# Opening of a two-layer decoder step: prompt rows loaded in four transfers, parameters on two queues and turned second, first block interleaved with the turning

## What is computed

```python
def _rms(x, g):
    y = x * lax.rsqrt(jnp.mean(x * x, axis=-1, keepdims=True) + EPS)
    return y * g
...
h = _rms(x, norm_mix[0])
a, g, mq = jnp.split(h @ w_in_a[0], [C_A, 2 * C_A], axis=-1)
c, st = _causal_dwconv(a * jax.nn.sigmoid(g), ...)      # 31 taps
...
```

## Time and profile before

| what | value |
|---|---|
| median of 3 runs | 1501.5 us (1499.77 to 1501.58) |
| time of the profiled execution | 1501.87 us |
| its span in the trace | 1500.2 us |
| instructions | 28216 |
| PE busy | 1401.7 us (93%) |
| DVE busy | 947.8 us (63%) |
| ACT busy | 584.2 us (39%) |
| POOL busy | 154.8 us (10%) |
| mean granted clock of PE | 0.974 |

### The profile page before, as it was taken

The page is one execution under the profiler, slowest core; times in us unless marked ns, Lnnn a source line. Parts: engine busy times, 40 slices in busy tenths (PEclk is TensorE's granted clock), DMA queues, the critical chain, the costliest instruction groups (busy, mean ns, idle before and its releaser), DMA issues.

```text
span 1500.2 us, 28216 instructions
## 1 busy us (share of the span) xinstructions
PE 1401.7 (93%) x11004; PEld 1332.0 (89%) x11004; DVE 947.8 (63%) x1812; ACT 584.2 (39%) x991; POOL 154.8 (10%) x202
## 2 busy tenths in 40 slices
PE   5899877799999999999999988898999999999997
PEld 5799765599999999999987877777999999999997
DVE  5689987666663565366776657666666536653662
ACT  4644534534431232123556454554443313221332
POOL 2000203222000000000300332220200000000001
PEclk9899987899999999999999999999999999999999
DMA  8112323124222322232322443332332332223222
GB/s 234 43 57 57 104 80 89 30 85 140 85 84 86 97 85 85 85 95 67 111 61 81 129 115 110 85 93 83 101 97 84 86 95 87 84 85 95 86 69 71
DMA packets 223216, 134.89 MB, mean 90 GB/s; under 512 B 7739, under 2 KB 216336, under 8 KB 223063
## 3 DMA queue, kind: packets, MB, share of 16 engines
q1 hardware_dynamic: 214687, 111.32, 26.0%
q0 software_dynamic: 7840, 21.89, 4.9%
q10 hardware_dynamic: 584, 0.23, 0.1%
HBM read 126.19 MB, written 7.85 MB: 89 GB/s over the span
## 4 chain that ended last, share of the span: by engine, by line
PE 75%; DVE 14%; ACT 6%; issue 3%; ACTq 1%; DMA 0%; POOL 0%; DVEq 0%; POOLq 0%
PE acc L532 61%; PE acc L709 3%; DVE conv_out L1727 2%; PE psT L666 2%; DVE softmax_stats L2102 1%; PE psX L666 1%; DVE w_lo L1629 1%; ACT w_hi L1156 1%; PE psX L544 1%; ACT exps L1491 1%; PE acc L544 1%; DVE xa_lo L1664 1%; DVE root_row L1652 1%; DVE psX L2100 1%; DVE turned L1640 1%
## 5 line engine op out<-in xcount | busy, mean ns | idle before, releaser
L532 PE MATMUL acc<-xa_hi,w_hi 128*128 128x272 f32 x1760 | 370.7, 292 | 5.4 <-DVE w_lo L1629 5.4
L532 PE MATMUL acc<-xa_hi,w_lo 128*128 128x272 f32 x1760 | 365.4, 289 | 0.0
L532 PE MATMUL acc<-xa_lo,w_hi 128*128 128x272 f32 x1760 | 364.5, 289 | 0.0
L1156 ACT ACTIVATE w_hi<-w_raw 128x1024 fp32r<-128x1024 f32 (+1 forms) x202 | 206.8, 1024 | 341.6 <-PE acc L532 312.2
L1629 DVE TENSOR_TENSOR w_lo<-w_raw,w_hi 128x1024 fp32r<-128x1024 f32 (+1 forms) x202 | 239.9, 1188 | 80.2 <-ACT w_hi L1156 78.2
L532 PEld LDWEIGHTS acc<-xa_hi,w_hi 128*128 128x128 f32 x1760 | 278.1, 189 | 11.5 <-DVE w_lo L1629 5.9
L532 PEld LDWEIGHTS acc<-xa_lo,w_hi 128*128 128x128 f32 x1760 | 278.2, 190 | 0.0
L532 PEld LDWEIGHTS acc<-xa_hi,w_lo 128*128 128x128 f32 x1760 | 276.3, 190 | 0.0
L532 PE MATMUL acc<-xb_hi,w_hi 128*128 128x272 f32 x896 | 194.3, 298 | 2.0 <-DVE xb_lo L2048 2.0
L532 PE MATMUL acc<-xb_hi,w_lo 128*128 128x272 f32 x896 | 185.8, 289 | 0.0
L532 PE MATMUL acc<-xb_lo,w_hi 128*128 128x272 f32 x896 | 185.3, 288 | 0.0
(11 more groups left out here) (337 smaller groups left out, 1879.9 us busy)
## 6 DMA issues: line engine op xcount, KB each, us to landing
w_raw<-in_w_up SPq DMA_DIRECT2D x88, 512.0 KB, 3.8
w_raw<-in_w_down SPq DMA_DIRECT2D x32, 512.0 KB, 3.9
w_raw<-in_w_in_a SPq DMA_DIRECT2D x14, 512.0 KB, 4.2
w_raw<-in_w_down SPq DMA_DIRECT2D x16, 384.0 KB, 3.4
w_raw<-in_w_kv SPq DMA_DIRECT2D x12, 512.0 KB, 4.0
k_pages<-in_cache_k POOLq DMA_DIRECT2D x96, 64.0 KB, 2.3
v_pages<-in_cache_v SPq DMA_DIRECT2D x96, 64.0 KB, 2.1
w_raw<-in_w_mem_kv SPq DMA_DIRECT2D x8, 512.0 KB, 3.8
```

Source lines behind the costliest of these rows:

```text
L532: last = nc.tensor.matmul(acc[slot][:, c, 0:n], w, x[:, k, c * n:(c + 1) * n], start=(k == 0 and q == 0), stop=(k == kb - 1 and q == 2))
L1156: nc.scalar.activation(whi[:, slot % 2, 0:n], wraw[:, slot, 0:n], ACT.Copy).then_inc(w_hi_ready, 1)
```

## The change

The prompt rows are loaded in four transfers of 256 columns instead of two of 512, each with a semaphore of its own, and the sample rows have one too. Every second of the 16 transfers of `put` is issued by POOL instead of ACT. PE turns the parameters after chunk 0 instead of after chunk 3, and turns chunks 4 to 7 inside step 0: chunk k + 4 before the products of chunk k. DVE alternates copies and low parts. ACT makes all high parts before any square, and its squares 0 to 7 follow w_hi(1).

```diff
@@ SP
-            sp.dma_start(xnat[0:NSA, QB, :], a["x_sample"]...).then_inc(ld_x[0], 16)
-            sp.dma_start(xnat[:, 0:QB, 0:512], x_rows[:, :, 0:512]).then_inc(ld_x[0], 16)
-            sp.dma_start(xnat[:, 0:QB, 512:D], x_rows[:, :, 512:D]).then_inc(ld_x[1], 16)
+            sp.dma_start(xnat[0:NSA, QB, :], a["x_sample"]...).then_inc(ld_xs, 16)
+            for i in range(4):
+                sp.dma_start(xnat[:, 0:QB, i * 256:(i + 1) * 256], x_rows[:, :, i * 256:(i + 1) * 256]).then_inc(ld_x[i], 16)
@@ PE
+            def turn_rows(c):
+
+                if c == 1:
+                    pe.wait_ge(ld_rows, 16 * (sum(1 for x in put[0::2] if x[2] is not None) + 4))
+                    pe.wait_ge(ld_rows2, 16 * sum(1 for x in put[1::2] if x[2] is not None))
+                    b = setup_bank(2)
+                    for i in range(4):
+                        n = min(P, NROW - i * P)
+                        last = nc.tensor.transpose(b[:, i * P:i * P + n], rows[0:n, i, :], ident[0:n, 0:n])
+                    last.then_inc(setup_filled, 1)
+                pe.wait_ge(ld_x[c // 2], 16)
+                b = setup_bank(1 + c + (c >= 1))
                 for i in range(QB):
                     last = nc.tensor.transpose(b[:, i * P:(i + 1) * P], xnat[:, i, c * P:(c + 1) * P], ident)
                 last.then_inc(setup_filled, 1)
...
+            for c in range(AHEAD):
+                turn_rows(c)
+
+            def first_ready(k):
+                if k + AHEAD < KD:
+                    turn_rows(k + AHEAD)
+                xa_ready(0)(k)
+
+            mm_step(0, 0, xa_hi, xa_lo, ready=first_ready)
             model_square_sum("n0")
@@ ACT
-            for r, k, src, done in put:
+            for r, k, src, done in put[0::2]:
...
-            for c in range(PARAMS_AT):
-                act.wait_ge(setup_drained, c + 2)
-                square(xT[:, c, :])
-            act.wait_ge(setup_drained, PARAMS_AT + 2)
+            act.wait_ge(setup_drained, 3)
             for c in range(KD):
-                if c == PARAMS_AT:
+                if c == 2:
                     split_hi(0)
-                if c >= PARAMS_AT:
+                if c >= 1:
                     act.wait_ge(setup_drained, c + 3)
                 scaled_hi(xa_hi, c, xT[:, c, :], pcol("norm_mix", c), xg_hi)
-            for c in range(PARAMS_AT, KD):
-                if c == PARAMS_AT + 2:
-                    split_hi(1)
+            split_hi(1)
+            for c in range(KD):
                 square(xT[:, c, :])
@@ DVE
+            row_copy(0)
+            dve.wait_ge(setup_filled, 3)
+            nc.vector.tensor_copy(pT[:, 0:NROW], psT[:, 0, 0:NROW]).then_inc(setup_drained, 1)
+            row_copy(1)
+            for c in range(2, KD):
+                if c == AHEAD:
+                    split_lo(0)
+                first_low(c - 2)
+                row_copy(c)
+            first_low(KD - 2)
+            first_low(KD - 1)
             split_lo(1)
@@ POOL
+            for r, k, src, done in put[1::2]:
+                if src is not None:
+                    pool.dma_start(rows[r % P:r % P + k, r // P, :], src[done:done + k, :]).then_inc(ld_rows2, 16)
```

More of the change, by code:

```diff
@@ L230, in build @@
         ld_const, ld_rows, ld_state, ld_mem = (sem(n) for n in ("ld_const", "ld_rows", "ld_state", "ld_mem"))
-        ld_x = [sem(f"ld_x{i}") for i in range(2)]
+        ld_xs, ld_rows2 = sem("ld_x_sample"), sem("ld_rows_pool")
+        ld_x = [sem(f"ld_x{i}") for i in range(4)]
         w_loaded = [sem(f"w_loaded{i}") for i in range(4)]
@@ L318, in build @@
         RT = dict(n0=0, mem=1, ln=2, n1=3, n2=4, n3=5)
-        PARAMS_AT = KD // 2
+        AHEAD = 4
         tiles = {}
@@ L425, in _ @@
             x_rows = a["x_prompt"].rearrange("o (i p) n -> (o p) i n", p=P)
-            sp.dma_start(xnat[0:NSA, QB, :], a["x_sample"].rearrange("b t n -> (b t) n")).then_inc(ld_x[0], 16)
-            sp.dma_start(xnat[:, 0:QB, 0:512], x_rows[:, :, 0:512]).then_inc(ld_x[0], 16)
-            sp.dma_start(xnat[:, 0:QB, 512:D], x_rows[:, :, 512:D]).then_inc(ld_x[1], 16)
+            sp.dma_start(xnat[0:NSA, QB, :], a["x_sample"].rearrange("b t n -> (b t) n")).then_inc(ld_xs, 16)
+            for i in range(4):
+                sp.dma_start(xnat[:, 0:QB, i * 256:(i + 1) * 256], x_rows[:, :, i * 256:(i + 1) * 256]).then_inc(ld_x[i], 16)
             def load(s, src, kb=KD):
@@ L580, in setup_bank @@
                 return psT[:, q % 2, :]
-            pe.wait_ge(ld_x[0], 32)
+            pe.wait_ge(ld_xs, 16)
             b = setup_bank(0)
@@ L587, in _, with xa_ready @@
             last.then_inc(setup_filled, 1)
-            for c in range(KD):
-                if c == PARAMS_AT:
-                    pe.wait_ge(ld_rows, 16 * (sum(1 for x in put if x[2] is not None) + 4))
-                    b = setup_bank(1 + c)
+            def xa_ready(n):
+                return lambda k: pe.wait_ge(xg_lo, 8 * n + k + 1)
+            def turn_rows(c):
[3 more added lines that the diff above has]
+                    b = setup_bank(2)
                     for i in range(4):
@@ L595, in _ @@
                     last.then_inc(setup_filled, 1)
-                    pe.wait_ge(ld_x[1], 16)
-                b = setup_bank(1 + c + (c >= PARAMS_AT))
+                pe.wait_ge(ld_x[c // 2], 16)
+                b = setup_bank(1 + c + (c >= 1))
                 for i in range(QB):
@@ L600, in _ @@
                 last.then_inc(setup_filled, 1)
-            def xa_ready(n):
-                return lambda k: pe.wait_ge(xg_lo, 8 * n + k + 1)
-            mm_step(0, 0, xa_hi, xa_lo, ready=xa_ready(0))
+            for c in range(AHEAD):
[5 more added lines that the diff above has]
+            mm_step(0, 0, xa_hi, xa_lo, ready=first_ready)
             model_square_sum("n0")
@@ L1670, in _, with row_copy, first_low @@
                                   ).then_inc(setup_drained, 1)
[L1671 to L1675, removed]
+            def row_copy(c):
+                i = 1 + c + (c >= 1)
                 dve.wait_ge(setup_filled, i + 1)
                 nc.vector.tensor_copy(xT[:, c, 0:NPR], psT[:, i % 2, :]).then_inc(setup_drained, 1)
-            dve.wait_ge(setup_drained, KD + 2)
-            for c in range(KD):
-                if c == PARAMS_AT:
+            def first_low(c):
+                if c == 0:
+                    dve.wait_ge(setup_drained, 3)
+                else:
+                    dve.wait_ge(setup_drained, c + 3)
+                scaled_lo(xa_lo, xa_hi, c, xT[:, c, :], pcol("norm_mix", c), xg_hi, xg_lo, c + 1)
+            row_copy(0)
[4 more added lines that the diff above has]
+                if c == AHEAD:
                     split_lo(0)
-                scaled_lo(xa_lo, xa_hi, c, xT[:, c, :], pcol("norm_mix", c), xg_hi, xg_lo, c + 1)
+                first_low(c - 2)
+                row_copy(c)
+            first_low(KD - 2)
+            first_low(KD - 1)
             split_lo(1)
```

## The result

The changed kernel takes 1510.66 us (median of 4 runs, 1509.47 to 1511.11) against 1500.63 for the kernel before (1499.61 to 1501.58). The ratio is 1.0066, with a 95% interval of 1.0048 to 1.0083: slower by 10.0 us. The profiled execution has a span of 1509.1 us against 1500.2, 8.9 more; its time, 1511.11 against 1501.87, is 9.2 more, so 0.3 us of it lies outside the span.

A forecast was written before the change was run, and what follows sets the result against it. Opening bound by parameter landing, then ACT and DVE, afterwards PE (93% busy). Sum 7.1 us later plus 2.1 for the low clock gives 9.2 on 1501.5: 1510.7 us, range 1505.5 to 1514.5.

The forecast's parts named there:

- The parameters' moment P: When PE's wait for the last parameter transfers ends: 15.23 before, taken as 13, the middle of 10.6 and 15.2.
- the rival with P counting as 10.6: Parameters land soon after issue, at 9.4 to 10.6; step 0's weights then decide; 6.8 us slower, 1508.3; chance 0.2.
- no gain (15.2): Rival: parameters land no earlier than before because queued data decides; 11.4 us slower, 1512.9; chance 0.15.
- its 6.05: Time in us from ACT's issue of the last parameter transfer to its landing in the kernel before.
- From P to the first square: Opening on PE, DVE and ACT, through the high parts until w_hi(1) ends and squares can start: P + 16.05 us.
- The squares' chain: Eight squares on ACT and POOL's additions behind w_hi(1), ahead of PE's sum: 10.65 us.
- The start of the sum: PE's sum over `square_total` between steps 0 and 1 starts at P + 26.7, 39.7 against 32.59: 7.1 us later.
- The sum at the low clock: PE's clock falls while idle, so the sum runs slower (1.9) and step 1 starts slower (0.2): 2.1 us.
- the 0.2 for step 1: Cost in us of step 1's start on PE until the clock is back, 4.2 us after work was taken up.
- What follows is moved as a whole: The stretch from 40.3 to 60 and all after it shift with the sum; nothing there takes the delay up.
- The rival of a better clock behind step 1: Not slower: clock at 1.00 in the stretch 40.3 to 60 shortens it by at most 5.1 us; chance 0.03.
- The price of moved work beside other work: POOL additions cost 1.32 to 1.41 us beside idle or copying DVE, 1.81 beside low parts; allowance -0.5 to +2.4 over six.

The follow-up runs named there:

- Experiment 1: Changed kernel with its squares spread over ACT's idle time in the opening instead of all behind w_hi(1); 1502.13 us, ratio 1.0008 to the kernel before.
- experiment 6: Changed kernel with POOL's second to sixth addition of the first norm cut from 544 to 8 columns; 1504.44 us, ratio 1.0030 to the kernel before.
- experiment 7: Changed kernel with 68 turnings of the identity on PE between step 0 and the sum; 1509.27 us, ratio 1.0058 to the kernel before.
- experiment 2: Kernel before with squares 0 to 7 all behind w_hi(1), nothing else changed; 1507.09 us, ratio 1.0043 to the kernel before.
- experiment 3: Changed kernel with PE's sum of squares behind step 1 instead of ahead of it; 1510.33 us, ratio 1.0064 to the kernel before.
- experiment 8: Changed kernel without late squares: parameters turned behind chunk 3, squares 0 to 3 before high parts, all chunks turned before step 0, DVE reordered; 1495.82 us, ratio 0.9965.
- experiment 5: Changed kernel with all eight chunks turned on PE before step 0, DVE and ACT unchanged; 1508.12 us, ratio 1.0055 to the kernel before.

## Why the prediction was right

The predicted 1510.7 us met 1510.66. The mechanism was right; that the number fits so closely is luck. The kernel before took 1500.63 in this comparison and not the 1501.5 that the prediction stood on, so the difference is 10.0 us (7.2 to 12.5 by the interval) against 9.2 predicted, and terms of the sum offset each other. In the profiled executions it is 6.0 for the later sum, 2.9 behind it and 0.3 outside the span. By its own steps:

- *The parameters' moment P.* Taken as 13, it was 12.83, and 12.2 to 13.1 in the seven experiments that have the change's loads and show PE waiting for them. No row gave it: it was the middle between two bounds, so the fit is luck. The last transfer on ACT was issued within 5.48 + 0.70 and took over 6.6 us to land, so neither early landing (the rival with P counting as 10.6) nor no gain (15.2) came true. Counted as the prediction counts its 6.05 (which is 6.1: 15.23 less 9.1), it took 7.0. The Trainium skill, page "DMA: Bandwidth & Descriptors", section on queues, rings and completion order, says that a DMA engine takes the queues that have work in turn, a packet at a time. The conclusion drawn from it, that P would follow the issue and count as 10.6, isn't borne out by this trace (12.83); what held the transfer no run shows.
- *From P to the first square.* Taken as 16.05 us, it was 15.0 (12.83 to 27.85), which put the sum 1 us too late. The turnings inside step 0 were priced too high: 0.85 each by the earlier trace rows, where four chunks took 3.40, but 0.42, 0.71, 0.71 and 0.36 from one row's start to the next in the changed kernel (19.56, 20.93, 23.15 and 24.78). The products between them took longer than assumed, 3.4 us for three chunks, where the prediction's times leave 2.9. w_lo(0) was done 0.3 us earlier after P than assumed.
- *The squares' chain.* Taken as 10.65 us, it was 10.72 (27.85 to 38.57). Experiment 1, which moves the chain, takes the wait out, and experiment 6, which shortens it, halves it. That the wait is at this chain's end is shown. One remark on it was wrong: not four squares and three additions ran before P in the kernel before, but two squares and one addition. Squares 2 and 3 start at 15.11 and the next two additions at 15.85, so a part of the cover was the turning and copying behind P.
- *The start of the sum.* 39.7 predicted, 38.57 measured: 6.0 us later than before, not 7.1.
- *The sum at the low clock.* This term was mis-sized: 2.1 predicted, 2.8 by experiment 7 and 2.9 by the traces (10.79 against 7.85 from the start of the sum to the memory rows). The two sums gave 1.8 of it, for the 1.9 predicted (38.57 to 41.97, against 32.59 to 34.22). The wrong part was the 0.2 for step 1: it took 7.39 us from its start to the memory rows instead of 6.22, 1.2 more, since its first rows too were at the low clock (0.50 from 42 to 44, 0.87 from 44 to 46).
- *What follows is moved as a whole.* 8.9 us at the memory rows, 8.9 in the span. The rival of a better clock behind step 1 did not occur: the granted clock was 0.74 from 49 to 69, as from 40.3 to 60 before.
- *The price of moved work beside other work.* The forecast needed it only for the changed kernel, where the additions run beside idle engines. Where it mattered, in experiments 1 and 2, I had it too low by some 2 us each.

What the change meant to gain was there: step 0 ended 3.6 us earlier, more than the 2.5 predicted. It was lost because all of the squares' chain moved behind it.

## What to carry to other kernels

Work that runs in the shadow of a wait has no cost until the wait is shortened or the work is moved out of it; before moving it, add up the whole serial chain it feeds, here eight squares and six additions, 10.7 us. Where a consumer stands between two long blocks, it matters when its input is complete, and moving the consumer alone gave nothing here (experiment 3). A wait on PE costs its length and what the clock loses behind it, here 2.8 us on 9.4; the table below shows that this second part didn't follow the length of the wait.

## What the runs showed of the hardware

**What a wait of PE cost behind it.** The stretch from the start of the sum to the memory rows holds the same work in these kernels, one execution of each (us):

| kernel | PE's wait before the sum | sum to memory rows |
|---|---|---|
| before | none | 7.85 |
| experiment 8 | none | 7.85 |
| experiment 7 | 1.98, behind 68 turnings | 7.95 |
| experiment 1 | 0.70 and 0.78, inside step 0 | 9.47 |
| experiment 5 | 6.09 | 9.64 |
| experiment 6 | 4.48 | 10.11 |
| changed | 9.42 | 10.79 |
| experiment 2 | 3.66 | 10.80 |

In the last five the granted clock was at 0.50 for most of the sum, in the first three at 1.00. The cost, 1.6 to 3.0 us, didn't grow with the wait; what sets it within these bounds stays open.

**The column of the granted clock can't be read alone.** In experiment 7 it reads 1.00 for the stretch from 20 to 24, while the rows of PE are at half pace: the row behind the four turnings at 21.82 starts 0.71 us after them (their duration is 1.05), in the changed kernel behind those at 24.78 only 0.36 us after them (0.60). The stretch (columns as in the earlier trace rows) and the timeline of experiment 7:

```profile
20.00:24.00 4.00, 4.00 (x20) 4.00 (x19) 2.66 (x5) 1.11 (x2) 0.00 (x0) 1.00 1.04 161
```

```profile
21.82 1.05 PE L607 MATMUL psT<-consts,x_rows 128*128 128x128 f32 x4
22.53 0.80 PE L534 MATMUL acc<-xa_hi,w_hi 128*128 128x272 f32 x2
```

In the executions looked at this occurs only ahead of the first fall that the column shows; whether a record is missing there or never made stays open. The pace of equal rows should be read beside it.

**Small transfers beside large ones.** A parameter transfer of half a kilobyte took over 6.6 us to land on ACT's queue, which held little else, while SP's transfers were under way. On POOL's queue the first transfer took 3.4 us and the last one of parameters 5.8. The changed kernel's transfers up to 30 us (operation, count, KB each, us to landing):

```profile
param_rows<-in_norm_ffn POOLq DMA_DIRECT2D x1, 8.0 KB, 3.4
...
param_rows<-in_subln_g POOLq DMA_DIRECT2D x1, 0.5 KB, 5.8
```
